# A two-stack sequence model on one core: Hyena's filter matmuls inside the down projection, both spectra by parity, the gated product and the sine argument in PSUM

## The reference, cut to what matters

```
x = x + 0.5 * _swiglu(_rmsnorm(x, ffn1_norm[i]), ffn1_w_gate[i], ffn1_w_up[i], ffn1_w_down[i])
proj = _rmsnorm(x, mix_norm[i]) @ w_in[i]
o_dn = _deltanet_group(...)          # gated delta rule, both directions
o_hy = _hyena_group(...)             # two long convolutions by FFT
x = x + jnp.concatenate([o_dn, o_hy], axis=-1) @ w_out[i]
x = x + 0.5 * _swiglu(_rmsnorm(x, ffn2_norm[i]), ffn2_w_gate[i], ffn2_w_up[i], ffn2_w_down[i])
```

```
hdn = jnp.sin(fr * (feats @ w1 + b1))
hdn = jnp.sin(fr * (hdn @ w2 + b2))
hdn = jnp.sin(fr * (hdn @ w3 + b3))          # 256 positions x 64
filt = (hdn @ wout).reshape(l, HY_DIRS, HY_ORDER, HY_WIDTH)
filt = filt * jnp.exp(-t * deltas)[:, None, None, :]
two_sided = jnp.concatenate([fwd, zeros, jnp.flip(bwd[: l - 1], axis=0)], axis=0)
return jnp.fft.rfft(two_sided, axis=0)
```

## Time and profile before

| | us |
|---|---|
| median of 3 runs (lowest, highest) | 1993.33 (1991.63, 1993.42) |
| the profiled execution, its own time | 1991.4 |
| its span | 1989.6 |
| TensorE busy in the span | 1952.2 |
| GpSimd, ScalarE, VectorE busy | 1491.4, 1038.4, 956.7 |

### The profile page before, as it was taken

The page is one execution under the profiler, slowest core; times in us unless marked ns, Lnnn a source line. Parts: engine busy times, 40 slices in busy tenths (PEclk is TensorE's granted clock), DMA queues, the critical chain, the costliest instruction groups (busy, mean ns, idle before and its releaser), DMA issues. The chain is left out here.

```text
span 1989.6 us, 37005 instructions
## 1 busy us (share of the span) xinstructions
PE 1952.2 (98%) x15763; PEld 1799.0 (90%) x15763; DVE 956.7 (48%) x1605; ACT 1038.4 (52%) x1551; POOL 1491.4 (75%) x652
## 2 busy tenths in 40 slices
PE   7999999999999999999999999999999999999998
PEld 7998788989989998788899989999999899999997
DVE  3560778343305550778343204845585038356750
ACT  5443456464436444456564437455644374656442
POOL 6789455469887889446278887768789877687896
PEclk9999999999999999999999999999999999999999
DMA  6756333136555756333145574545555645455653
GB/s 223 248 181 206 110 107 127 42 114 207 184 199 172 226 183 202 102 107 107 45 149 191 191 231 151 168 149 191 170 191 192 208 155 166 146 190 168 194 197 127
DMA packets 250965, 329.09 MB, mean 165 GB/s; under 512 B 9008, under 2 KB 225586, under 8 KB 250418
## 3 DMA queue, kind: packets, MB, share of 16 engines
q1 hardware_dynamic: 250802, 326.73, 50.6%
HBM read 325.66 MB, written 1.05 MB: 164 GB/s over the span
## 5 line engine op out<-in xcount | busy, mean ns | idle before, releaser
L1020 POOL TENSOR_TENSOR w_lo<-raw,w_hi 128x1024 fp32r<-128x1024 f32 x600 | 1455.7, 2444 | 480.4 <-ACT w_hi L597 478.9
L410 PE MATMUL psA<-xT_hi,w_lo 128*128 128x256 f32 x3168 | 896.3, 283 | 8.1 <-POOL w_lo L1020 4.2
L411 PE MATMUL psA<-xT_lo,w_hi 128*128 128x256 f32 x3168 | 883.8, 279 | 0.0
L412 PE MATMUL psA<-xT_hi,w_hi 128*128 128x256 f32 x3168 | 883.8, 279 | 0.0
L597 ACT ACTIVATE w_hi<-raw 128x1024 fp32r<-128x1024 f32 x600 | 630.3, 1052 | 360.4 <-PE psB L412 237.6
L410 PEld LDWEIGHTS psA<-xT_hi,w_lo 128*128 128x128 f32 x3168 | 599.2, 189 | 22.2 <-issue 11.4
L411 PEld LDWEIGHTS psA<-xT_lo,w_hi 128*128 128x128 f32 x3168 | 595.6, 188 | 2.5 <-issue 2.4
L412 PEld LDWEIGHTS psA<-xT_hi,w_hi 128*128 128x128 f32 x3168 | 597.4, 189 | 0.0
L1166 DVE TENSOR_TENSOR hT_lo<-hfull,hT_hi 128x256 fp32r<-128x256 f32 x132 | 214.8, 1659 | 2.8 <-ACT hT_hi L730 1.4
L410 PE MATMUL psB<-w_hi,hT_lo 128*128 128x512 f32 x528 | 205.6, 389 | 1.4 <-issue 1.4
L412 PE MATMUL psB<-w_hi,hT_hi 128*128 128x512 f32 x528 | 205.5, 389 | 0.0
(11 more groups left out here) (446 smaller groups left out, 2319.3 us busy)
## 6 DMA issues: line engine op xcount, KB each, us to landing
raw<-in_w_in SPq DMA_DIRECT2D x78, 1024.0 KB, 5.1
raw<-in_ffn_w_gate SPq DMA_DIRECT2D x44, 1024.0 KB, 5.1
raw<-in_ffn_w_up SPq DMA_DIRECT2D x44, 1024.0 KB, 5.2
raw<-in_ffn_w_down SPq DMA_DIRECT2D x44, 1024.0 KB, 4.8
raw<-in_w_ffn_in SPq DMA_DIRECT2D x44, 1024.0 KB, 5.0
raw<-in_w_ffn_out SPq DMA_DIRECT2D x22, 1024.0 KB, 4.8
raw<-in_w_out SPq DMA_DIRECT2D x16, 1024.0 KB, 4.8
raw<-in_w_branch_da SPq DMA_DIRECT2D x4, 1024.0 KB, 4.8
```

Source lines behind the costliest of these rows:

```text
L410: nc.tensor.matmul(o, a_lo, b_hi, start=start, stop=False, skip_group_check=skip)
L411: nc.tensor.matmul(o, a_hi, b_lo, start=False, stop=False, skip_group_check=skip)
L412: return nc.tensor.matmul(o, a_hi, b_hi, start=False, stop=stop, skip_group_check=skip)
L1020: nc.gpsimd.tensor_tensor(split_half(w_lo, n, kind), raw_half(n, kind), split_half(w_hi, n, kind).bitcast(F32), ALU.subtract)\
```

## The change

It does six things.

1. `hdn` and `wfilt` get 128 rows: rows 64 to 127 hold a second copy of the third sine and the weights of the backward direction. The filter matmuls of forward and backward direction stand one behind the other, on the array's upper and lower 64 rows, in different psA banks.
2. These matmuls stand in the down projection of FFN 1: the first order's four behind block 4, the second's behind block 9. VectorE's 18 filter instructions stand ahead of `add_to_x`, all on psA.
3. Both spectra are formed by parity, four matmuls for each order (`filter_spectra`), right behind the down projection, the second into psB. ScalarE copies the first's parts to `parity`, VectorE adds and subtracts them (`first_spectrum`). Behind projection 3 TensorE has nothing of them left; VectorE's `second_spectrum` stays there.
4. The gated product is written over the up product in psA, and `hT_hi` and `hT_lo` read it there. The next up projection waits for `hT_lo` (`f_lo`) instead of the product.
5. The sine's argument is formed in psB bank 3 and `farg` in eight instructions, each with an operand in PSUM, and the sine reads PSUM; ScalarE takes it ahead of its two roundings of the step.
6. The fourth key group goes from behind projection 25 to behind projection 26.

SP issues 23 parameter loads per layer instead of 20 (two more rows of 64 values, and the filter weights in two parts).

The diff, without the buffer addresses and the parameter loads:

```diff
@@ act, ffn and mlp_sin
+                    if st == 0 and f == 0 and j in (6, 8, 10):
+                        mlp_sin(l, j // 2 - 3)
                     for i in range(2):
...
-                        A(hT_hi[:, n, :], hfull[:, i, :], ACT.Copy).then_inc(f_hi[st].sem, 1)
-                    if st == 0 and f == 0 and j in (6, 8, 10):
-                        mlp_sin(l, j // 2 - 3)
+                        A(hT_hi[:, n, :], psA[:, 2 + i, 0:L], ACT.Copy).then_inc(f_hi[st].sem, 1)
...
-                A(hdn[:, 1:L + 1], farg[:, 0, :], ACT.Sin).then_inc(s1["mlp_sin"].sem, 1)
+                n = P if k == 2 else HID
+                A(hdn[0:n, 1:L + 1], psB[0:n, 3, 0:L], ACT.Sin).then_inc(s1["mlp_sin"].sem, 1)
...
-                    A(spec[:, 0, k, :], psA[:, k, :], ACT.Copy).then_inc(s1["spec"].sem, 1)
+                    A(parity[:, k, :], psA[:, k, :], ACT.Copy).then_inc(s1["spec"].sem, 1)
@@ dve, ffn and mlp_argument
-                        if n >= 2:
-                            dve.wait_ge(f_lo[st].sem, f_lo[st].due(l, NF * f + n - 1))
-                        V.tensor_tensor(hfull[:, i, :], sg[:, i, :], psA[:, 2 + i, 0:L], ALU.mult).then_inc(f_prod[st].sem, 1)
+                        V.tensor_tensor(psA[:, 2 + i, 0:L], sg[:, i, :], psA[:, 2 + i, 0:L], ALU.mult).then_inc(f_prod[st].sem, 1)
...
-                        V.tensor_tensor(hT_lo[:, n, :], hfull[:, i, :], hT_hi[:, n, :].bitcast(F32), ALU.subtract)\
+                        V.tensor_tensor(hT_lo[:, n, :], psA[:, 2 + i, 0:L], hT_hi[:, n, :].bitcast(F32), ALU.subtract)\
...
-                a, n = farg[:, 0, :], farg[:, 1, :]
+                m = P if k == 2 else HID
+                a, b, n = farg[0:m, :], psB[0:m, 3, 0:L], psB[0:m, 3, L:2 * L]
...
-                V.tensor_scalar(a, psB[0:HID, 3, 0:L], cols[0:HID, 113 + k:114 + k],
-                                                cols[0:HID, 116:117], ALU.add, ALU.mult).then_inc(ch.sem, 1)
+                V.tensor_scalar(a, b, cols[0:m, 113 + k:114 + k], cols[0:m, 116:117], ALU.add, ALU.mult)
+                V.tensor_scalar(b, b, cols[0:m, 113 + k:114 + k], cols[0:m, 116:117], ALU.add, ALU.mult).then_inc(ch.sem, 1)
...
-                    V.scalar_tensor_tensor(a, n, -c, a, ALU.mult, ALU.add).then_inc(ch.sem, 1)
+                    V.scalar_tensor_tensor(b if c == c3 else a, n, -c, a, ALU.mult, ALU.add).then_inc(ch.sem, 1)
@@ dve, spectra and order
+            def first_spectrum(l):
+
+                dve.wait_ge(s1["spec"].sem, s1["spec"].due(l, 4))
+                for c in range(2):
+                    e, o = parity[:, 2 * c, :], parity[:, 2 * c + 1, :]
+                    V.tensor_tensor(spec[:, 0, 2 * c, :], e, o, ALU.add).then_inc(s1["odd"].sem, 1)
+                    V.tensor_tensor(spec[:, 0, 2 * c + 1, :], e, o, ALU.subtract).then_inc(s1["odd"].sem, 1)
...
             def stack1_projections(l):
...
-                filters(l, 1)
+                first_spectrum(l)
...
                 ffn(0, l, 0, 0)
+                filters(l, 0)
+                filters(l, 1)
                 add_to_x(0, l, 0, 65, None)
-                filters(l, 0)
                 norm_scale(0, l, 1)
@@ pe
+                    if n in filters_behind:
+                        filters(l, filters_behind.index(n))
...
-                            pe.wait_ge(f_prod[st].sem, f_prod[st].due(l, NF * f + 2 * (j - 1) + i + 1))
+                            pe.wait_ge(f_lo[st].sem, f_lo[st].due(l, NF * f + 2 * (j - 1) + i + 1))
...
-                into_x(st, l, s0 + 2 * NF, hT_hi, hT_lo, f_lo[st], NF * f)
+                into_x(st, l, s0 + 2 * NF, hT_hi, hT_lo, f_lo[st], NF * f, filters_behind=(4, 9) if st == 0 and f == 0 else ())
...
+            def filters(l, o):
+
+                if o == 0:
+                    pe.wait_ge(s1["mlp_sin"].sem, s1["mlp_sin"].due(l, 3))
+                    pe.wait_ge(f_lo[0].sem, f_lo[0].due(l, NF))
+                else:
+                    pe.wait_ge(s1["odd"].sem, s1["odd"].due(l, 2))
+                for rb in range(RB):
+                    for d in range(DIRS):
+                        r, t0 = slice(HID * d, HID * (d + 1)), rb + 1 - d
+                        M(psA[:, 2 * rb + d, :], hdn[r, t0:t0 + L - 1:2], wfilt[r, o, :], start=True, stop=True)\
+                            .then_inc(s1["filt_mm"].sem, 1)
+
+            def filter_spectra(l):
+
+                pe.wait_ge(tables_loaded, 32)
+                pe.wait_ge(s1["odd"].sem, s1["odd"].due(l, 4))
+                for o in range(2):
+                    if o:
                         pe.wait_ge(x_ready[0].sem, x_ready[0].due(l, 4))
+                    for b in range(4):
+                        src = filt[o][:, b % 2, :] if b >= 2 else even[o][:, b % 2, :]
+                        M((psA, psB)[o][:, b, :], dft_f[:, b // 2 + b % 2 * 2, :], src, start=True, stop=True)\
+                            .then_inc(s1["spec_mm"].sem, 1)
...
-                    pe.wait_ge(s1["odd"].sem, s1["odd"].due(l, 8))
+                    pe.wait_ge(s1["odd"].sem, s1["odd"].due(l, 12))
...
-                    if i == 3:
-                        second_spectrum(l)
...
                         turn_rows_kv(l, 0)
+                    if i == 26:
                         key_products(l, 3)
-                    if i == 26:
                         turn_rows_kv(l, 1)
```

More of the change, by code:

```diff
@@ L233, in emit @@
         root_row = at("root_row", 98, [P, L])
-        hfull = at("hfull", 46, [P, 2, L])
         xn = at("xn", 87, [P, RB, D])
@@ L238, in emit @@
         spec = at("spec", 0, [P, 2, 4, HYW])
-        filt = at("filt", 20, [P, RB, 2, HYW])
+        filt = [at("filt0", 54, [P, RB, HYW]), at("filt1", 67, [P, RB, HYW])]
+        parity = at("parity", 20, [P, 4, HYW])
         qkvT = at("qkvT", 20, [P, 12, L])
@@ L491, in layer_params1 @@
                         param(rows[113 + n:114 + n, 0:HID], ins[name][bass.ds(l, 1)])
+                        if n >= 2:
+                            param(rows[113 + n:114 + n, HID:P], ins[name][bass.ds(l, 1)])
                     param(fw[0:EMB, 0, :], layer(ins["hy_f_w1"], l))
@@ L1810, in project_two, with into_x @@
                 ins_.then_inc(half_used[st].sem, 2)
-            def into_x(st, l, s0, a_hi, a_lo, made=None, counted=0, blocks=None, last=False):
+            def into_x(st, l, s0, a_hi, a_lo, made=None, counted=0, blocks=None, last=False, filters_behind=()):
                 whole = blocks is None
@@ L1905, in second_spectrum @@
-            def second_spectrum(l):
-                pe.wait_ge(s1["odd"].sem, s1["odd"].due(l, 4))
-                for b in range(4):
-                    src = filt[:, b % 2, 1, :] if b >= 2 else even[1][:, b % 2, :]
-                    M(psB[:, b, :], dft_f[:, b // 2 + b % 2 * 2, :], src, start=True, stop=True).then_inc(s1["spec_mm"].sem, 1)
+            def filters(l, o):
+                if o == 0:
+                    pe.wait_ge(s1["mlp_sin"].sem, s1["mlp_sin"].due(l, 3))
+                    pe.wait_ge(f_lo[0].sem, f_lo[0].due(l, NF))
+                else:
+                    pe.wait_ge(s1["odd"].sem, s1["odd"].due(l, 2))
+                for rb in range(RB):
+                    for d in range(DIRS):
+                        r, t0 = slice(HID * d, HID * (d + 1)), rb + 1 - d
+                        M(psA[:, 2 * rb + d, :], hdn[r, t0:t0 + L - 1:2], wfilt[r, o, :], start=True, stop=True)\
+                            .then_inc(s1["filt_mm"].sem, 1)
@@ L2356, in _ @@
                 ffn(0, l, 0, 0, 0)
-                filters(l)
+                filter_spectra(l)
                 turn_x(0, l, 1)
```

53 lines of the change are left out of this document (18 added, 35 removed).

## The result

| | before | changed |
|---|---|---|
| median, both kernels run side by side, us | 1993.38 | 1965.26 (lowest 1964.45, highest 1966.77) |
| ratio, 95% interval | | 0.9856 (0.984 to 0.9872) |
| own time of the profiled execution | 1991.4 | 1966.77 |
| its span | 1989.6 | 1965.0 |

The forecast was 1977, with a range of 1970 to 1985. Between medians the change is worth 28.1 us, between the two profiled executions 24.6; the forecast's sum was 16.0. The medians in this document leave out two executions, one of `restart_mm` at 5762.86 us and one of the kernel before at 3991.66.

What follows compares the result with a forecast made beforehand. TensorE, busy 1952.2 of 1989.6 us, was taken to bound the kernel. Two layers at -5.2 (-10.4) and FFN -5.6 gave -16.0, so 1975.4 profiled and 1977 median; range 1970 to 1985.

Steps and rivals of the forecast that it cites:

- FFN term: TensorE's FFN waits, 4.2 us for `w_lo` and 1.4 unnamed, all go: -5.6 once, bounds -3.5 and -6.
- Join: Between FFN 1 and mixer: filters leave, 16 spectrum records stay, norm starts earlier; -7.0 us per layer, bounds -6.3 and -7.4.
- Filters in the down projection: Eight filter matmuls return as four side-by-side pairs in two groups; +4.1 us per layer, bounds 3.6 and 7.5.
- Second spectrum: Behind projection 3, four matmuls go: -3.5 us; 0.5 back at Hyena transposes, 0.7 at decay sums, per layer.
- rival 2: At the projections' start, VectorE's four `parity` sums of 2.5 us come too late: +7.6, 1985; chance 0.14.
- rival 4: Up projections' wait for `hT_lo` decides from each FFN's second step: slower, 30 us at 0.5 beyond, 2007; chance 0.04.
- Key group: Last key group in the mixer: `yb` wait goes, but TensorE meets the masks earlier; 0, bounds -1.6 and +0.8 us.
- FFN 2 and stack 2 have hardly a stall to lose: nothing: In FFN 2 and stack 2, moving product and sine argument to PSUM gains nothing.
- one cadence, 0.117: In the projections, a TensorE matmul takes 0.117 us, so 24 matmuls take 2.8 us.

Runs made afterwards that it cites:

- restart_mm: Changed kernel plus one unused fp32 matmul of 128 columns at each of five places in the FFNs; medians 1970.62 and, run again, 1971.22 us.
- hyena_only: Changed kernel with gated product and sine argument back in SBUF, up projections waiting for the product again; 1980.23 us, ratio 0.9934.

## Why the prediction was wrong

The mechanisms that the forecast named came as it said, one by one. The size of the FFN term was off, and the pace, which the forecast took for one figure, was put at nothing.

- **Join**: forecast -7.0 per layer, measured -7.3 (9.20 for 16.51). The transposes wait for neither `xn` nor the spectra's copies.
- **Filters in the down projection**: forecast +4.1, measured 2 x 2.15 = +4.3 at the two groups; the whole down projection is 4.2 longer. Of a group's 2.0 us two pairs are 1.72, so 0.3 are for going in and out, as the row of the scores had it. The rule of the Trainium skill (TensorEngine Tiling (Array Packing), Key Properties), that a change of tiling mode drains the engine, agrees with that: from the last product to the first filter matmul on 64 rows it is 0.32 us, to the first spectrum matmul on all rows 0.23.
- **Second spectrum**: forecast -3.5 and 1.2 given back, measured -3.4 and 0.6, so -2.8. The Hyena transposes wait 0.5 (the row with `spec` above), as forecast; the 0.7 ahead of the decay sums did not come, they wait no longer than before. Per layer the three make -5.9.
- **`parity`** (rival 2): the four sums take 0.68, 2.89, 2.88 and 0.68 us in layer 0, 7.1 for the 5 to 6 of the forecast, and nothing waits for them. **`hT_lo`** (rival 4): no up projection waits for it. The rule of the Trainium skill (SBUF — State Buffer, Who interferes with whom), as the prediction gives it, holds here: `hT_lo` takes 1659 ns with two SBUF inputs beside GpSimd, 421 with one, 1690 in `hyena_only` with two again.
- **Key group**: forecast 0, measured 0.
- **The step that failed**: "I take all of 4.2 + 1.4: -5.6 once". It is the term of the FFNs. It measured -8.7, and the pace, a term that the forecast did not have, moved another -4.9 in the profiled pair, together -13.6. So there are two reasons.
  First, the view of waits gives idle time, from the end of one record to the start of the next. In this stream, where the records overlap, a pause costs more than that. Before the stall of rows 6 the trace of the kernel before has

```profile
97.96 0.28 PE L412 MATMUL psA<-xT_hi,w_hi 128*128 128x256 f32 x1
```

  and the next product at 100.62: 2.66 from start to start, where 0.113 was due, and 0.08 more until the restarted stream is at its pace. That is 2.63 for an idle time of 2.38. There were 13 such pauses in the six FFNs, with 6.1 us of idle time. From start to start, with the slow first matmuls behind each, all pauses there come to 10.9 us, of which the 2.2 at groups of other matmuls stayed. The 5.6 of the two rows were a part of the smaller figure. "FFN 2 and stack 2 have hardly a stall to lose: nothing" was wrong for the same reason: 1.8 us were there.
  Second, the pace. The forecast had one cadence, 0.117 for a matmul of 256 columns, read off a slow stretch. The changed kernel ran 1090 fewer matmuls at the slower pace, worth 4.9 us in the profiled pair; that fewer pauses and a shifted count of records did it is likely, and not shown. The other timed runs have no trace; that the remaining 3.5 us between -24.6 and -28.1 are pace as well is likely by the table above, and not shown.
- The range was built from the bounds of the terms, without a term for what the other executions of the same code do. One FFN more or less at the slower pace is 4.5 us.

## What to carry to other kernels

Price a pause of TensorE from start to start against the cadence, and add up all of them, small ones too; the view of waits shows the least of it. Before a difference of a few us is explained, count how many matmuls ran at which distance in both traces: it differed here in stages whose code was the same. A VectorE instruction between two SBUF tensors that stands beside GpSimd's work and ahead of a later wait is worth a bank of PSUM for one of its operands, even where VectorE itself has time: here that was 5.7 to 8.2 of some 20 us at one pace, the smaller half of the gain, and the half that the forecast had too small.

## What the runs showed of the hardware

- A stream of 128x256 matmuls, each with its own weight load, has two steady distances, 113.3 and 117.8 ns, at full granted clock. Streams of 128x512 ran at 226.7 ns throughout. The Trainium skill (TensorE: Matmul & The Clock Gate, Back-to-back issue gap) gives columns over 2.4 GHz and some 2.5 ns for a single gap, which makes 109 ns at 256 columns by estimate, and about 131 ns for a stream with weight loads at 512 columns. Neither is what these traces show, and the traces decide.
- Which of the two it is turned with a small group inserted without a wait by its number of records: two turned it (47 of 47), four kept it (40 of 40), one gave slow, slow, slow, fast in turn. It may turn at a pause (28 of 76). Why the kernel's own groups behave otherwise, the four fp32 matmuls behind step 4 among them, is open.
- Behind one pause of 2.2 us the clock was at its lower level for 3.4 us (0.213 us a matmul); behind one of 2.66 at the same place in another execution it was not.
- Two 64-row fp32 matmuls on different halves of the array run side by side: 1.99 us for eight, 3.71 for the same eight on one half.
- A VectorE subtraction of 128x256 takes 1659 ns in the mean with both inputs in SBUF beside GpSimd's splits, and 421 with one of them in PSUM.
